# Low parts of eight weight units of the third FFN: by VectorE's subtraction, or by a transfer that adds onto a stored negative

## The reference

```python
D_FF_2 = -(-8 * D_MODEL // (3 * 256)) * 256   # 2816
    h = rms_norm_2(x, norm_ffn_pre_g[l])
    f = (jax.nn.silu(h @ w_gate[l]) * (h @ w_up[l])) @ w_down[l]
    x = x + rms_norm_2(f, norm_ffn_post_g[l])
```

## Time and profile before

| | us |
|---|---|
| median of 3 runs | 1885.31 |
| lowest, highest | 1883.43, 1885.83 |
| the profiled execution, its own time | 1883.09 |
| its span in the profile | 1881.3 |
| TensorE busy | 1869.5 (99%) |
| VectorE, ScalarE, GpSimd busy | 927.4 (49%), 719.6 (38%), 145.2 (8%) |

### The profile page before, as it was taken

One profiled execution on the slowest core, in us unless ns is written; L12 is line 12 of the kernel. 1 busy time (PEld: TensorE's weight loads), 2 busy tenths in 40 slices (PEclk: granted clock), 3 DMA queues, 4 the chain that ended last, 5 costly groups with the idle time before them and its releaser, 6 DMA issues.

```text
span 1881.3 us, 23862 instructions
## 1 busy us (share of the span) xinstructions
PE 1869.5 (99%) x9422; PEld 1538.1 (82%) x9422; DVE 927.4 (49%) x1240; ACT 719.6 (38%) x990; POOL 145.2 (8%) x130
## 2 busy tenths in 40 slices
PE   9999999999999999999999999999999999999998
PEld 7888888887778888888888888777888998888887
DVE  4444431456686555644443227554656474444323
ACT  6223221364534444423222125444665462232222
POOL 0000000124430200200000003000000000000000
PEclk9999999999999999999999999999999999999999
DMA  6343332232214232333332224333332333333222
GB/s 180 89 109 91 89 107 94 90 112 81 69 55 157 71 108 90 92 110 89 90 110 90 89 90 131 108 101 101 106 105 70 90 90 99 101 89 98 104 90 79
DMA packets 214306, 184.18 MB, mean 98 GB/s; under 512 B 7685, under 2 KB 192090, under 8 KB 214234
## 3 DMA queue, kind: packets, MB, share of 16 engines
q1 hardware_dynamic: 213536, 183.13, 31.9%
q10 hardware_dynamic: 698, 0.05, 0.0%
HBM read 172.67 MB, written 2.10 MB: 93 GB/s over the span
## 4 chain that ended last, share of the span: by engine, by line
PE 95%; DVE 2%; ACT 1%; issue 1%; POOL 0%; DVEq 0%; ACTq 0%; POOLq 0%
PE bank L564 26%; PE bank L566 26%; PE bank L565 26%; PE bank L784 6%; PE bank L626 2%; PE bank L628 2%; PE bank L627 2%; PE bank L1082 1%; ACT w_hi L1184 1%; PE bank L1066 1%; PE bank L1052 1%; PE bank L1051 0%; DVE w_lo L1739 0%; PE bank L844 0%; DVE n_lo L1748 0%
## 5 line engine op out<-in xcount | busy, mean ns | idle before, releaser
L1739 DVE TENSOR_TENSOR w_lo<-w_raw,w_hi 128x2048 fp32r<-128x2048 f32 x160 | 368.0, 2300 | 704.5 <-ACT w_hi L1184 704.3
L564 PE MATMUL bank<-n_hi,w_hi 128*128 128x512 f32 (+1 forms) x1792 | 706.4, 394 | 1.5 <-DVE n_lo L1849 1.1
L566 PE MATMUL bank<-n_hi,w_lo 128*128 128x512 f32 (+1 forms) x1792 | 691.6, 386 | 0.0
L565 PE MATMUL bank<-n_lo,w_hi 128*128 128x512 f32 (+1 forms) x1792 | 691.4, 386 | 0.0
L1184 ACT CAST w_hi<-w_raw 128x2048 fp32r<-128x2048 f32 x160 | 305.5, 1909 | 594.3 <-PE bank L566 501.3
L564 PEld LDWEIGHTS bank<-n_hi,w_hi 128*128 128x128 f32 x1792 | 336.7, 188 | 71.3 <-issue 4.4
L566 PEld LDWEIGHTS bank<-n_hi,w_lo 128*128 128x128 f32 x1792 | 336.6, 188 | 68.8
L565 PEld LDWEIGHTS bank<-n_lo,w_hi 128*128 128x128 f32 x1792 | 336.9, 188 | 66.8 <-issue 3.4
L564 PE MATMUL bank<-h_hi,w_hi 128*128 (+1 forms) x352 | 137.1, 390 | 0.2
L566 PE MATMUL bank<-h_hi,w_lo 128*128 (+1 forms) x352 | 137.0, 389 | 0.0
L565 PE MATMUL bank<-h_lo,w_hi 128*128 (+1 forms) x352 | 136.9, 389 | 0.0
(11 more groups left out here) (310 smaller groups left out, 1866.9 us busy)
## 6 DMA issues: line engine op xcount, KB each, us to landing
w_raw<-in_w_in SPq DMA_DIRECT2D x68, 512.0 KB, 4.6
w_raw<-in_ffn_down SPq DMA_DIRECT2D x44, 512.0 KB, 3.9
w_raw<-in_ffn_gate SPq DMA_DIRECT2D x43, 512.0 KB, 4.0
w_raw<-in_ffn_up SPq DMA_DIRECT2D x43, 512.0 KB, 5.2
w_raw<-in_w_gate SPq DMA_DIRECT2D x22, 512.0 KB, 4.0
w_raw<-in_w_up SPq DMA_DIRECT2D x22, 512.0 KB, 5.1
w_raw<-in_w_down SPq DMA_DIRECT2D x22, 512.0 KB, 4.2
w_raw<-in_w_kv_mem SPq DMA_DIRECT2D x16, 512.0 KB, 4.5
```

Of the source, the lines that this page charges most:

```text
L564: pe.matmul(acc, w_hi, x_hi, start=start, stop=False)
L565: pe.matmul(acc, w_hi, x_lo, start=False, stop=False)
L566: return pe.matmul(acc, w_lo, x_hi, start=False, stop=stop)
L1739: dve.tensor_tensor(wlo[par][:, :], raw[par][:, :], whi[par][:, :].bitcast(F32), ALU.subtract).then_inc(w_lo_ready, 1)
```

## The change

For down units 2 to 9 of the third FFN the low part is made in another way. ScalarE, after rounding the unit into `w_hi`, waits for its own write and runs a second pass that writes -`w_hi` into `w_lo`, and counts up `w_neg`. GpSimd waits for that and issues a transfer that reads the unit's weights from HBM a second time and adds them to what stands in `w_lo`, which gives `w_raw` - `w_hi`; it counts `w_added` by 16. VectorE no longer subtracts. It waits for `w_added` and writes a zero into one column of `small` that nobody reads, only to count up `w_lo_ready`, on which TensorE and SP wait as before. SP still loads each unit into `w_raw`, from which ScalarE makes the high part. The loops of ScalarE and VectorE are written out for this FFN. Units 0, 1 and 10 and all others are as before.

```diff
+        w_neg, w_added = sem("w_neg"), [sem("w_added0"), sem("w_added1")]
...
+            down3 = a["w_down_2"][0].rearrange("(k p) n -> p k n", p=P)
+            for n in range(2, DOWN_UNITS - 1):
+                pool.wait_ge(w_neg, n - 1)
+                pool.dma_start(wlo[(U_FFN3 + GATE_UNITS + n) % 2][:, :].rearrange("p (k n) -> p k n", k=2),
+                               down3[:, 2 * n:2 * n + 2, :], accum_op=ALU.add).then_inc(w_added[n % 2], 16)
...
-                with act.Fori(0, (DOWN_UNITS - 3) // 2) as i:
-                    for j in range(2):
-                        split((b + j) % 2, i + (b + j) // 2)
+                if f == 2:
+                    for n in range(DOWN_UNITS - 3):
+                        split_unit(b + n)
+                        act.wait_ge(w_hi_ready, b + n + 1)
+                        act.activation(wlo[(b + n) % 2][:, :], whi[(b + n) % 2][:, :].bitcast(F32), ACT.Copy, scale=-1.0).then_inc(w_neg, 1)
+                else:
+                    with act.Fori(0, (DOWN_UNITS - 3) // 2) as i:
+                        for j in range(2):
+                            split((b + j) % 2, i + (b + j) // 2)
...
-                with dve.Fori(0, (DOWN_UNITS - 3) // 2) as i:
-                    for j in range(2):
-                        split((b + j) % 2, i + (b + j) // 2)
+                if f == 2:
+                    for n in range(DOWN_UNITS - 3):
+                        dve.wait_ge(w_added[n % 2], 16 * (n // 2 + 1))
+                        dve.memset(small[:, (20 if n < 4 else 72) + n:(21 if n < 4 else 73) + n], 0.0).then_inc(w_lo_ready, 1)
+                else:
+                    with dve.Fori(0, (DOWN_UNITS - 3) // 2) as i:
+                        for j in range(2):
+                            split((b + j) % 2, i + (b + j) // 2)
```

## The result

The changed kernel takes 1895.33 us (median of 5 runs, 1894.74 to 1898.05), the kernel before 1885.43 us (5 runs beside it). The ratio is 1.0055 with a 95% interval of 1.004 to 1.007: slower by 9.9 us. The forecast was 1896.0 us, slower by 10.7.

A forecast was written before the change was run, and what follows sets the result against it. TensorE bounds the kernel. Each chain, 3.88 + 9.35 + 0.25 us, exceeds 10.8 by 2.7; paid at four units, 10.7 us on 1885.3 gives 1896.0 us, range 1884.0 to 1925.0.

The forecast's parts named there:

- The bound: Third FFN's down products: TensorE's matmuls set the time; the eight subtractions taken from VectorE, 18.3 us, are worth 0.
- The chain: Per changed unit, split start to TensorE: 3.88 us to the issue, transfer 9.35, relay 0.25, against 10.8 us available.
- wake-up of GpSimd: GpSimd starting after ScalarE's negative: 0.03 us, taken as from ScalarE to VectorE.
- issue to steady data (unit 2): Start of GpSimd's transfer: 1.65 us to first data as in SP's load, plus 1.6 us for GpSimd's issue.
- steady data (unit 2): Data time of the adding transfer: the plain load's 2.9 us doubled to 5.9 by reading the negative too.
- X, issue to landing: GpSimd's adding 1 MB transfer, issue to semaphore: 9.35 us central, 4.8 low, 13.7 high; hidden below 6.7.
- landing, by way of VectorE, to TensorE: After the transfer VectorE wakes, writes one column, and TensorE wakes: 0.25 us.
- Half the rate: The adding transfer reads the negative from SBUF besides the weights, so data time doubles to 5.9 us.
- The pattern: Units 2, 4, 6 and 8 stall by 2.7 us each; odd units get their time from the stall before.
- The sum: Four stalls of 2.7 us on TensorE add 10.7 us, giving 1896.0 us.
- my limit of 10.8 us: Time from a split's start within which the low part must reach TensorE, else TensorE waits.
- The clock: Clock stays at 1.00, as 2.7 us stalls are under 3.1; rival: it falls, 1902 or at worst 1983 us, chance 0.05.

The follow-up runs named there:

- two kernels with one parity: Changed kernel with the transfer only at units 2, 4, 6, 8 (ratio 1.006) or only at 3, 5, 7, 9 (1.0047); VectorE subtracts for the others.
- The plain transfer: Changed kernel with accum_op=ALU.add taken away, so the weights overwrite the negative; ratio 0.9999 to the kernel before.
- The kernel with the odd units: Changed kernel with only units 3, 5, 7, 9 by transfer, the others by VectorE's subtraction; ratio 1.0047 to the kernel before.
- the one with early gains: Changed kernel with the 512 KB gains load moved from SP's queue to ScalarE's, ahead of unit 2's split; ratio 1.0049 to the kernel before.
- the two with the negative first: Changed kernel with ScalarE writing the negative before the high part: ratio 1.0028 alone, 1.0013 with the gains also loaded early.
- the one from SBUF: Changed kernel with the whole-unit transfer adding from w_raw in SBUF instead of HBM; ratio 1.0031 to the kernel before.
- the one with the even units: Changed kernel with only units 2, 4, 6, 8 by transfer, the others by VectorE's subtraction; 1895.02 us, ratio 1.006.
- half-unit kernel from SBUF: Changed kernel with only each unit's second 1024 columns by negative and transfer, from w_raw in SBUF; VectorE subtracts the first; ratio 0.9996.
- the one with all three edits: Changed kernel with negative written first, gains loaded early and whole-unit transfer from SBUF; ratio 1.0002 to the kernel before.

## Why the prediction was right

**The bound** was read rightly: with everything hidden, the stretch is TensorE's own time and nothing that left VectorE was worth anything.

**The chain** of an even unit, forecast as 3.88 + 9.35 + 0.25 = 13.48 us, measured at unit 4 from 1792.44 to 1805.09: 12.65 us. Its terms, at unit 4 where no other unit is named:

| term | forecast, us | measured, us |
|---|---|---|
| second pass on ScalarE | 1.91 | 1.92 |
| wake-up of GpSimd | 0.03 | 0.29 |
| issue to steady data (unit 2) | 3.25 | 3.4 |
| steady data (unit 2) | 5.9 | 4.6 |
| end of the data to landing (unit 2) | 0.2 | 0.7 |
| X, issue to landing | 9.35 | 8.3 |
| landing, by way of VectorE, to TensorE | 0.25 | 0.17 |

Half the rate was right: some 205 GB/s, which is 5.1 us for the megabyte, against 410 to 437. The size was off by a reading of mine as well: the slices of the earlier trace rows have data from 1783.25 to 1785.95, 2.7 us and not 2.9, and the double of that is 5.4. The Trainium skill's page "Collectives: The Full Stack" (The bandwidth ceiling: the fold count and why AG ≠ RS ≠ AR) says of ReduceScatter, an operation between cores, that it has half the rate of AllGather because its addition needs two source reads. The trace agrees with the half, 205 against some 420 GB/s; no run here shows the second read. The Trainium skill's page "DMA: Bandwidth & Descriptors" (Anatomy of one DMA — SWDGE (gpsimd) path) has about 2.0 us plus the bytes at 436 GB/s, an estimate of 4.4 us here. The plain transfer took 5.3 us and the adding one 8.4 us; the measurement decides.

**The pattern**, a stall paid at every second unit, was right, and the two kernels with one parity show it. A fifth gap, ahead of unit 9, was not forecast.

**The sum was right partly by cancellation.** (1) The gaps were 2.23, 1.86, 1.75 and 1.81 us, not 2.7: 7.65 us against 10.7. (2) Each gap moves the next split by 0.3 us more than its length (2.23 against 13.42 - 10.88 = 2.54): the four moved it by 2.54, 2.16, 2.09 and 2.11, 8.9 us. Half of the 0.3 us is how idle time is counted: matmuls start 0.23 us apart and last 0.39, so the slot of the next one is lost from 0.16 us before the gap begins, and my limit of 10.8 us, which ended with the last matmul, was too long by that. Another 0.11 us is the first matmul behind a gap: from its start to that of the third are 0.56 us (1781.16 to 1781.72), where 0.45 are usual (1777.86 to 1778.31). Neither was a term of my sum. (3) Unit 9 cost another 1.6 us, which I had not seen: SP's queue sends the 512 KB of gains right behind unit 10's weights, and they met unit 9's transfer (9.9 us). I had looked for collisions with the weights alone. (4) 0.2 us at units 5 and 7. Together 8.9 + 1.6 + 0.2 = 10.7 us, 10.65 by the stretch. The median's 9.9 us differs from this by less than the 1.7 us by which the start of an execution varies. So a transfer forecast some 1 us too long made up for a wake-up of GpSimd, a restart and a fifth stall that I had too short or not at all: that the sum meets the measured one within 0.1 us is luck.

**The clock** stayed at 1.00 through all five gaps of this execution, but the argument for it was too good. I took the 3.1 us of the earlier trace rows as if no shorter stop could lower it. The kernel with the odd units and the one with early gains had a 3.4 us low stretch each, after gaps of 2.19 and 1.96 us; the other sixteen gaps of 1.7 to 2.3 us in the profiles here had none. So such a stall costs 1.7 us now and then; the eight gaps of 3.9 to 6.3 us all cost 1.6 us or more.

## What to carry to other kernels

Work that moves to an idle engine or queue is free only up to the slack of the chain that it is in. That slack can be read off as the distance between two splits minus the chain before. Nothing is gained where the engine that sets the time did not wait. With two slots a late chain is paid every second unit, so half of the late work can be undone with little back (1.7 of 10.65 us here), and a few microseconds cut from the chain (a pass taken out of it, a nearer source, another queue's load moved away) give all of it back. Look down every queue past the transfers at hand: here a gain vector's load was the fifth stall.

## What the runs showed of the hardware

- A transfer that adds onto SBUF moves about 205 GB/s from HBM, half of the plain rate, and no more from SBUF (203). GpSimd needs 1.19 us to issue 256 rows with addition, 0.72 us without, 0.85 us for 128 rows with it. From SBUF as the source, with 128 rows of 8 KB, the megabyte lands 1.3 us sooner (7.1 against 8.4).
- TensorE's clock fell to the 1.2 GHz level at two of eighteen pauses of 1.7 to 2.3 us and at all eight of 3.9 to 6.3 us. Behind the four of 3.9 to 4.1 us it fell 0.3 to 1.2 us after work was taken up again and came back 3.4 us later; in the four of 5.8 to 6.3 us it fell inside the pause and came back 6.8 us later.
- A pause of TensorE costs 0.3 us more than the profile's idle time: 0.16 us because matmuls that overlap are counted to their ends, 0.11 us for the first matmul behind it.
- In several kernels the transfer of unit 6 was up to 1.9 us longer than its neighbours; the cause is open. In the plain-transfer kernel the stretch of 1815 to 1822 has a fetch of instructions beside it, and the data end in a tail of 23 GB/s, the rate of one of sixteen engines:

```profile
GB/s 0 0 0 0 0 0 0 234 304 23 0 0 328 468 351 351 421 398 492 398 398 374 374 421 375 164 23 23 23 23 47 23 23 23 0 0 0 0 0 0
...
q8 instruction: 1, 0.02, 0.8%
...
w_lo<-in_w_down POOLq DMA_DIRECT2D x1, 1024.0 KB, 6.7
```

The next two transfers, with no fetch beside them, landed in 5.2 us. The other traces are divided. In this kernel, the two with the negative first and the one from SBUF the fetch begins 2.5 to 6.9 us after the issue of unit 6's transfer, while its data run, and that transfer is 0.7 to 1.9 us longer than its neighbours. In the changed kernel, the one with the even units and the one with early gains it begins 1.3 to 1.5 us after the issue, ahead of the stream, and unit 6's transfer takes 8.3 to 8.4 us like the others. But in the half-unit kernel from SBUF and the one with all three edits unit 6's transfer is 0.6 and 0.7 us longer, though the fetch begins only as its data end. No run moved a fetch, so that it holds up one engine's share stays open.
